# The attention of the first block spread over one stream of weight parts, a head every three slots

## What is computed

```python
proj = rms_norm(x) @ w_in                      # q (16 heads), k, v (4 heads), u, gate_a, gate_b
q, k = rms_norm(q, q_norm_g), rms_norm(k, k_norm_g)       # a head of 128 columns each
y_a  = windowed_gqa(q, k, v, attn_sink) @ w_attn_o         # per head, 256 x 256 scores, ALiBi, sink
y_b  = (y_act @ glu_w_a) * sigmoid(y_act @ glu_w_b)        # y_act: the state-space branch
merged = sigmoid(gate_a) * y_a + sigmoid(gate_b) * y_b
x = x + merged @ w_out
```

## Time and profile before

| what | value |
|---|---|
| median of 3 runs | 3993.94 us (3990.68 to 3995.81) |
| profiled execution | 3992.67 us, span 3990.9 us |
| TensorE busy (share of the span) | 2447.9 us (61%) |
| VectorE, ScalarE, GpSimd busy | 2199.8, 1252.7, 2657.1 us |
| mean granted clock of TensorE | 0.804 of full speed |

### The profile page before, as it was taken

The page is one execution under the profiler, slowest core; times in us unless marked ns, Lnnn a source line. Parts: engine busy times, 40 slices in busy tenths (PEclk is TensorE's granted clock), DMA queues, the critical chain, the costliest instruction groups (busy, mean ns, idle before and its releaser), DMA issues.

```text
span 3990.9 us, 35652 instructions
## 1 busy us (share of the span) xinstructions
PE 2447.9 (61%) x11418; PEld 2021.6 (51%) x11418; DVE 2199.8 (55%) x2700; ACT 1252.7 (31%) x1773; POOL 2657.1 (67%) x1192
## 2 busy tenths in 40 slices
PE   6899977998410110100000008999999999889997
PEld 5788755777300100100000006888888888768775
DVE  7788222131799999999999984222232222221322
ACT  4666544444200000000000003444434444333553
POOL 5200333876587877878788886777787777666555
PEclk9999987998755555555555558999999999988998
DMA  5444422664699999999999995555555555444444
GB/s 162 131 125 131 134 84 70 183 190 150 251 420 381 418 405 383 417 407 422 378 422 422 405 399 162 164 171 162 164 173 165 170 163 167 134 159 137 132 127 142
DMA packets 238655, 935.94 MB, mean 235 GB/s; under 512 B 37664, under 2 KB 39840, under 8 KB 171680
## 3 DMA queue, kind: packets, MB, share of 16 engines
q0 software_dynamic: 73728, 536.90, 32.7%
q1 hardware_dynamic: 156576, 390.13, 32.2%
q10 hardware_dynamic: 8192, 6.90, 0.6%
HBM read 927.02 MB, written 2.10 MB: 233 GB/s over the span
## 4 chain that ended last, share of the span: by engine, by line
PE 55%; DVE 21%; issue 8%; POOL 7%; ACT 3%; DMA 3%; DVEq 2%; ACTq 1%; POOLq 0%
PE products L599 39%; PE products L1131 8%; DVE arena L2416 8%; DVE arena L2404 7%; POOL arena L2136 7%; DMA arena<-peer_up_in,arena 2%; DVE arena L946 1%; PE products L620 1%; PE products L888 1%; PE products L1905 1%; PE products L1880 1%; DMA arena<-peer_down_in,arena 1%; ACT weights_high L531 1%; PE products L911 1%; ACTq L1820 1%
## 5 line engine op out<-in xcount | busy, mean ns | idle before, releaser
L543 POOL TENSOR_TENSOR weights_low<-arena,weights_high 128x1024 fp32r<-128x1024 f32 x528 | 1287.1, 2445 | 625.3 <-ACT weights_high L531 624.2
L599 PE MATMUL products<-weights_high,input_high 128*128 128x512 f32 x2432 | 991.7, 408 | 555.4 <-DVE weights_low L543 533.1
L531 ACT ACTIVATE weights_high<-arena 128x1024 fp32r<-128x1024 f32 x612 | 645.7, 1059 | 1126.2 <-PE products L599 963.8
L599 PE MATMUL products<-weights_high,input_low 128*128 128x512 f32 x2432 | 963.3, 396 | 0.0
L599 PE MATMUL products<-weights_low,input_high 128*128 128x512 f32 x2432 | 963.0, 396 | 0.0
L599 PEld LDWEIGHTS products<-weights_high,input_high 128*128 128x128 f32 x2432 | 468.3, 193 | 654.8 <-DVE weights_low L543 326.3
L2416 DVE SCALAR_TENSOR_TENSOR arena<-arena 128x2048 f32<-128x2048 f32 x256 | 611.6, 2389 | 29.4 <-DMA arena<-peer_up_in,arena 4.4
L2136 POOL DMA_INDIRECT arena<-peer_down_in,arena x256 | 507.6, 1983 | 174.3 <-DVE arena L2404 88.1
L2136 POOL DMA_INDIRECT arena<-peer_up_in,arena x256 | 552.1, 2157 | 82.6 <-issue 80.0
L2404 DVE SCALAR_TENSOR_TENSOR arena<-arena 128x2048 f32<-128x2048 f32 x256 | 573.7, 2290 | 22.5 <-DMA arena<-peer_down_in,arena 20.1
L620 PE MATMUL products<-arena 128*128 128x128 f32 x248 | 58.0, 409 | 852.8 <-DVE arena L2436 720.2
(11 more groups left out here) (311 smaller groups left out, 2913.4 us busy)
## 6 DMA issues: line engine op xcount, KB each, us to landing
arena<-dsa_in SPq DMA_DIRECT2D x320, 512.0 KB, 3.5
arena<-w_in_in SPq DMA_DIRECT2D x128, 512.0 KB, 3.8
arena<-mla_wide_in SPq DMA_DIRECT2D x97, 512.0 KB, 3.5
arena<-w_attn_o_in SPq DMA_DIRECT2D x32, 512.0 KB, 3.6
arena<-w_out_in SPq DMA_DIRECT2D x32, 512.0 KB, 4.1
arena<-peer_w_query_in SPq DMA_DIRECT2D x32, 512.0 KB, 4.4
arena<-dsa_w_out_in SPq DMA_DIRECT2D x32, 512.0 KB, 3.6
arena<-glu_w_b_in SPq DMA_DIRECT2D x16, 512.0 KB, 3.7
```

The source lines that it names most:

```text
L531: nc.scalar.activation(w_hi[:, u % RING, :, at], ring[:, u % RING, :, at], ACT.Copy).then_inc(hi_made, 1)
L543: ops.tensor_tensor(w_lo[:, u % RING, :, at], ring[:, u % RING, :, at], w_hi[:, u % RING, :, at].bitcast(F32), op=ALU.subtract).then_inc(l ...
L599: mm = nc.tensor.matmul(PS[:, bank(b) + t, 0:width], x[:, x0 + n, at], y, start=n == 0 and m == 0, stop=n == len(parts) * PK - 1 and m == 2)
```

## The change

From the value slab to the output slabs there is now one list of slots on all engines, numbered a = 0 to 135: value (0 to 7), query (8 to 39), gated (40 to 71), attention output (72 to 103), output (104 to 135). In slot a every engine does what is due: TensorE one part (`a_part`) and then steps (`a_pe`), ScalarE the weight copy four parts ahead (`hi_part`) and then `a_act`, VectorE `a_dve`.

- Head h takes its scores in slot 20 + 3h (k = 0), exponentials and normalising in the next (k = 1), transposes at k = 3, values at k = 4. The last head's values are in slot 69.
- Key turns are in slots 2 and 3. Query slab i is rooted and scaled in slot 16 + 8i and turned in the second and third slot behind; QT, like the scaled rows, is kept twice.
- The gated slabs come before the attention-output slabs. The state-space output is split in slots 33 to 36. Four pairs of attention output are split to the upper half of XH and XL (slots 37, 38, 40 and 46), four to the lower half (69 to 72).
- After a gated slab VectorE makes GB = sigmoid(gate_b) y_b; after an attention-output slab it makes GB = GB + GA y_a, with a second pair of row buffers `gate_rows`.
- The merge is turned by quarters: turns 0 to 5 in slots 97 to 102, turns 6 and 7 in slots 105 and 106.
- v_quad, sinks_quad and the wait on v_staged go. SyncE waits before it loads x until all attention output is split. Loops on the engines become straight code.

```diff
-W_U, W_G, W_K, W_V, W_Q, W_O, W_GLU, W_OUT, W_PQ = 0, 2, 10, 11, 12, 16, 20, 24, 28
+W_U, W_G, W_K, W_V, W_Q, W_GLU, W_O, W_OUT, W_PQ = 0, 2, 10, 11, 12, 16, 20, 24, 28
+A_GLU, A_O, A_OUT = PARTS * (W_GLU - W_V), PARTS * (W_O - W_V), PARTS * (W_OUT - W_V)
+A_END = A_OUT + PARTS * 4
+A_FIRST, A_SPACE = 20, 3
+def a_heads(a):
+    for h in range(HEADS):
+        k = a - A_FIRST - A_SPACE * h
+        if 0 <= k <= 4:
+            yield h, k
+def a_turn(a):
+    i, m = divmod(a - 2 * PARTS, PARTS)
+    if a in (2, 3):
+        return a - 2
+    return 2 + 2 * i + m - 2 if 0 <= i < QUADS and m in (2, 3) else None
+def a_pair(a):
+    for u in range(HEADS // 2):
+        free = A_GLU - PARTS // 2 + u if u < PARTS // 2 else A_O - PARTS + u
+        if a == max(free + 1, A_FIRST + A_SPACE * (2 * u + 1) + 5):
+            return u
+def a_merged_turn(a):
+    u = a - (A_OUT - PARTS + 1)
+    if u in range(6):
+        return u
+    return u - 2 if u in (8, 9) else None
+def a_place(u):
+    return (u + PARTS // 2) % PARTS
...
+        def a_pe(pe, a):
+            for h, k in a_heads(a):
+                if k == 3:
+                    pe.wait_ge(p_ready, after(H_A + h))
+                    pe.wait_ge(pt_ready, 1 + h)
...
+                    tr.then_inc(p_turned, 1)
+                if k == 4:
...
+                    mm.then_inc(pv_made, 1)
+            for h, k in a_heads(a):
+                if k == 0:
...
+                    pe.wait_ge(turned, after(X_Q + 2 * i + c // 2))
+                    pe.wait_ge(score_read, 1 + h)
...
+                    mm.then_inc(score_made, 1)
+            j = a_turn(a)
+            if j is not None:
+                i, u = divmod(j - 2, 2)
+                moved(pe, B_K if j < 2 else B_Q + i)
...
+        def a_act(act, a):
+            for h, k in a_heads(a):
...
+            for h, k in a_heads(a):
+                if k == 1:
+                    act.wait_ge(bias_ready, after(H_A + h))
...
+            if a == 0:
+                head_roots_of(act, B_K, W_K, 0, v_rows)
...
+            i, m = divmod(a - 2 * PARTS, PARTS)
+            if 0 <= i < QUADS and m == 0:
+                head_roots_of(act, B_Q + i, W_Q + i, 0, ks_rows)
...
+        def a_dve(dve, a):
+            if a == 0:
+                scale_heads(dve, B_K, 0, 0, ks_rows)
+            i, m = divmod(a - 2 * PARTS, PARTS)
+            if 0 <= i < QUADS and m == 0:
...
+                scale_heads(dve, B_Q + i, 1, i, rows[:, i % 2])
+            for h, k in a_heads(a):
+                if k == 1:
+                    dve.wait_ge(exp_done, after(H_A + h))
...
+                    n.then_inc(p_ready, 1)
+            for h, k in a_heads(a):
+                if k == 0:
+                    dve.wait_ge(score_made, after(S_A + h))
...
+            sp.wait_ge(lhs_lo, L_AO + HEADS // 2)
             sp.dma_start(X, I["x"][0].rearrange("(t p) d -> p t d", p=P)).then_inc(x_in, 16)
...
+            for a in range(A_OUT + PARTS // 2):
+                hi_part(act, PARTS * W_V + a + RING)
+                a_act(act, a)
...
+            for a in range(A_END):
+                a_part(pe, a)
+                a_pe(pe, a)
```

More of the change, by code:

```diff
@@ L345, in program @@
         v_rows = cols.take(NT, NC)
-        v_quad = cols.take(NT, HD)
-        QT = cols.take(QUAD, SEQ)
+        QT = cols.take(2, QUAD, SEQ)
         PA = cols.take(2, NT, SEQ)
         PTA = cols.take(2, NC)
+        gate_rows = cols.take(2, NT, NC)
         H = G.rearrange("p t d -> p (t d)")[:, 0:NT * D].rearrange("p (t d) -> p t d", t=NT)
@@ L482, in program @@
         skip_ready, y_made, y_read, y_act = sem("skip_ready"), sem("y_made"), sem("y_read"), sem("y_act")
-        merged = sem("merged")
+        gated, merged = sem("gated"), sem("merged")
         out_done = sem("out_done")
@@ L685, in scale_heads @@
                 op=ALU.mult).then_inc(evac[b % 2], 2)
[L688 to L707, removed]
-                        mm = nc.tensor.matmul(PS[:, SCORE_BANK + s % 2, at:at + seen(t)], qq[:, t * P:(t + 1) * P],
-                                              kk[:, 0:seen(t)], start=n == 0, stop=n == len(pairs) - 1)
-                    at += seen(t)
-                mm.then_inc(score_made, 1)
@@ L2203, in _ @@
-            act.drain()
-            split_hi(act, W_O, 0, range(3, RING))
-            lhs_split_hi(act, YT, range(KT // 2))
-            with act.Fori(0, 4) as i:
-                feed(act, W_O, i)
-            made(act, W_O + 3)
-            act.wait_ge(ys_in, 16 * 8 * SSM_KT)
-            for u in range(SSM_KT // 2):
-                nc.scalar.activation(XH[:, 2 * u:2 * u + 2].rearrange("p k (j i) -> p k j i", i=CHUNK),
-                                     YS[:, 2 * u:2 * u + 2].rearrange("p k (i j) -> p k j i", i=CHUNK), ACT.Copy)\
-                    .then_inc(lhs_hi, 1)
@@ L2214, in _ @@
-            with act.Fori(0, 4) as i:
-                split_hi(act, W_GLU, i, range(RING, PARTS))
-                made(act, W_GLU, i, PARTS // 2 - 1)
-                act.wait_ge(merged, 1 + i)
-                nc.scalar.activation(rows[:, 0], PS[:, bank(0):bank(0) + 2], ACT.Sigmoid).then_inc(evac[0], 2)
-                split_hi(act, W_GLU + 1, i, range(RING))
-            turn_hi(act, X_MER)
+            for a in range(A_OUT + PARTS // 2):
+                hi_part(act, PARTS * W_V + a + RING)
+                a_act(act, a)
@@ L2232, in _ @@
                           allow_slow_non_contiguous=True).then_inc(pos_in, 16)
-            with act.Fori(0, 4) as i:
-                feed(act, W_OUT, i)
+            for a in range(A_OUT + PARTS // 2, A_END):
+                hi_part(act, PARTS * W_V + a + RING)
             act.wait_ge(evac[0], B_PQ)
```

401 lines of the change are left out of this document (173 added, 228 removed).

## The result

The kernel after takes 3890.26 us (median of four runs, 3884.87 to 3893.88) where the kernel before takes 3992.31 in the same comparison: a ratio of 0.9745, with a 95% interval of 0.9727 to 0.9763. The profiled execution took 3888.33 us. The prediction was 3889, with a range of 3872 to 3914.

What follows compares the result with a forecast made beforehand. TensorE was taken to wait on VectorE and ScalarE chains and run at slow clock; 411.9 us of work plus 16.5 of waits make 428.4 in place of 532.3, 103.9 less, giving 3889 us, range 3872 to 3914.

Steps and rivals of the forecast that it cites:

- (a): Key heads: ScalarE's roots and scaling take 6.4 us with the copy, against two slots (5.44); 1.2 us lost.
- (b): Slot 24: scaling before normalising makes head 1's transposes wait 5.5 us (3.1 least, 7.1 dear end), plus 1.7 clock: 7.2.
- (c): Slots 32 to 35: third query slab's scaling ahead of head 4's scores; 1.3 us wait plus 1.7 clock, 3.0.
- (d): Slots 33 to 40: split subtractions ahead of heads 5 and 6; one head late by 2, clock 1.6: 3.6 us.
- (e): Gated stage: slot 56 carries a gated evacuation and new scores; head 12 late by 0 to 3, taken as 1.5 us.
- clock term: Half-speed products after a TensorE stop, priced from one 2.24 us stop: 1.7 us, or 1.6, per restart.
- three stage ends: Starts of gated, attention-output and output slabs: they cost nothing any more, with no wait over 1 us.
- 16 heads: Attention heads: costed at nothing, as three slots hide each chain, with weights ready some 1.5 us before TensorE asks.
- Everything hidden: Rival: chains of later terms read too slow, TensorE stands only 0 to 8 us; 3872 to 3880, chance 0.22.
- Contention at every head: Rival, third listed case: VectorE meets GpSimd throughout, twelve more heads cost 1.6 us each; 3899 to 3918, chance 0.20.
- Only the stage ends gain: Rival: the attention stretch stays as long as today, only stage ends gain 31 us; 3961, chance 0.04.
- slower case: In-order wait at every head's transposes: slower if each is late by 5.8 us or more; 7 late gives 4012; chance 0.03.

Runs made afterwards that it cites:

- best2: Kernel after with scaling behind head steps, four further moves (key roots, state-space splits, gated step, fused normalising) and a head every two slots: 3875.42 us, 0.9723 of before.
- order: Kernel after with the scaling of a query slab put behind the heads' steps in VectorE's slot: 3883.41 us, 0.9738 of the kernel before.
- space2: Kernel after with a head every two slots in place of three, still three slots from scores to transposes: 3879.97 us, 0.9721 of the kernel before.
- nosink: Kernel after with the sink left out of the softmax denominators, dropping VectorE's small add: 3876.18 us, one run, no ratio.
- twoslots: Kernel after with a head's transposes two slots behind its scores, not three: 3957.07 us, 0.9922 of the kernel before.
- second repeat: Kernel after, unchanged, measured again with the last group of experiments: 3891.98 us, 0.9763 of the kernel before.
- ends: Kernel after with all splits of the left operands back at the stage ends (slots 39 and 71): 3906.18 us, 0.9783 of the kernel before.
- mergewhole: Kernel after with all eight merge turns at once in slot 103, ahead of the output slabs: 3900.36 us, 0.9765 of the kernel before.

## Why the prediction was right

**The whole.** The sum was 411.9 of work and 16.5 of waits; the stream took 430.2, 1.8 more than the 428.4. That it is so near is partly luck: the work was priced 4.4 us too low and the waits with their restarts 2.5 us too high (14.0 found), and the two errors partly cancel. The range was meant to reach to the upper edge of the third rival, but that edge is 3918, and 3914 was written; the measured time is far from either.

**The work** was too cheap by 4.4 us. Slots without steps keep the 2.72. A slot with one head's scores and another's transposes takes 4.05, one with values 3.63, so a head costs 1.33 + 0.91 = 2.24, not 2.14 (16 x 0.10 = 1.6). A slot with a merge turn takes 3.20, so a turn costs 0.48, not 0.42 (18 x 0.06 = 1.1). Both prices came from rows in which such steps stood side by side; between slab products each handover costs a little more. The other 1.7 was not found in one place. best2's 416.1, with 0.8 of waits, says the same: 3.4 over 411.9.

**(a) The key turn**: 1.2 forecast, 1.28 found, with no slow restart behind it.

**(b) Slot 26**: 7.2 forecast, 6.26 + 2.2 = 8.5 found. Between the ends I had taken 5.5 for the wait; it is 6.26, nearer to the dear end of 7.1, and the reason is the one given for that end: two of VectorE's steps each meet a subtraction. order and space2 show that scaling ahead of normalising makes the wait. The restart: transposes, scores, a turn and the first products from 518.76 to 523.51 at half pace, 2.2 above the full-clock distances of the other heads, where 1.7 was put.

The trace shows the small add, both inputs in SBUF, at 1.93 us beside GpSimd and at 0.16 alone. That agrees with the exclusive lock in SBUF — State Buffer, "SBUF: Two separate sides", of the Trainium skill, which the prediction left as the dearer case. nosink adds what that sentence alone doesn't give: taking one operation out of the row moves the meeting to the next.

ScalarE's switch of tables between the roots and the factors, in the same slot:

```profile
511.03 1.28 ACT L717 ACT_TABLE_LOAD   x1
512.32 0.30 ACT L717 ACTIVATE arena<-arena 128x8 f32<-128x8 f32 x1
```

It takes 1.29 to the next activation. The 2.66 of the Trainium skill (ScalarE: Activation LUTs, "What ACT_TABLE_LOAD costs") would have made (b) and (c) 1.4 later; the trace goes with the shorter price.

**(c) Slot 35**: 3.0 forecast, 0.98 found; **(d) slots 33 to 40**: 3.6 forecast, 1.58 + 0.27 found; **(e) slot 59**: 1.5 forecast, 1.36 found. The waits themselves were near (1.3 and 2 in the sum for (c) and (d)). The step that failed is the clock term that I added to each, 1.7 and 1.6: the rows behind these stops show transposes of 0.66 us at a distance of 0.49 to the scores, which is full pace (granted clock 1.00). What the rows of the changed streams show is this: behind stops of 0.98 to 2.09 us TensorE went on at the full clock; behind those of 3.08 and more it ran at half pace for a while, at a cost of 1.5 to 2.5 us where it was worked out here. Between them a stop's length doesn't tell: 2.39 and 2.40 lost the clock in twoslots, 2.49 and 2.51 kept it, and in the kernel before stops of 2.24 did both. Nor does the loss begin with the stop's end: behind the 3.77 of the second repeat the transposes and scores ran at full pace, and the granted clock was 0.50 only from 577.0 to 579.0. What decides was not found. I had one row, the 2.24 of the earlier trace rows, and applied it to every stop.

**What I costed at nothing.** The supply of parts: TensorE waits for no weight part in the stream, so it is right. The three stage ends: 86.70 busy of 86.70, and no wait at the output slabs; ends and mergewhole put 14.4 and 16.0 back, of which 13 and 11.1 are the stage ends themselves. The 16 heads: right in the result, since only the four late ones of (b) to (e) wait, but the spare 1.5 us per head was counted too high. twoslots takes 2.72 away and each head is 3.5 late on the mean, where 1.5 of spare would leave 1.2. The head shown above meets GpSimd twice and is 3 us longer for it; with a third slot such meetings stay hidden, and I had counted the chain from steps at their undisturbed lengths.

**The rivals.** Everything hidden falls with the 6.26 of slot 26; but best2 shows that it was to be had, at 416.1. Contention at every head falls with four late heads in place of 16. VectorE does meet GpSimd often (in nine of the 16 heads the add takes 0.84 us or more in place of 0.16), but the third slot hides it. With two slots of distance the rival becomes true. Only the stage ends gain falls with the attention's 0.99 in the window; twoslots, in which 36 of the 102 us remain, shows what it would have looked like: 3957.07, near the 3961 given for it. The slower case needed 5.8 us of lateness at each head; the mean with two slots is 3.5, so even one slot less still leaves a kernel 0.9922 of the one before.

**A miss of the experiments' own.** For space2 I expected a loss, because I looked at how dense the heads were and not at which slots they share with other steps. The cause of (b), known by then, would have given the sign: 21 + 2h and 24 don't meet.

**Left open**: why the stream starts at 432 to 434 us in some executions and at 438 to 439 in others, which moves a whole time by as much as some of these edits; why what follows the stream, which no experiment touches, takes anything from 3013.9 us (nosink) to 3028.3 (space2); and what decides whether TensorE loses its clock behind a stop of 2.2 to 2.5 us.

## What to carry to other kernels

Before a chain of small steps is put beside a stream of large products, write down for each slot and engine which steps meet there: one pair in the wrong order cost 9 us here, and either their order in the slot or the distance of the heads removed it. A distance between producer and consumer is cheap as long as the stream has work to fill it; count the chain with one operation of the other engine per step that can meet one, not with the steps' lengths alone, since one slot too few cost 66 us. Price a stop by what rows show behind stops of its own length, and look at more than one such row: here no stop of up to 2.09 us in the changed streams brought a half-speed restart, every one of 3.08 and more did, and of those between some did and some didn't. And repeat the trace of the unchanged kernel: one head there was 2.2 us later the second time.

## What the hardware did that I had not expected

VectorE and GpSimd take turns operation by operation, so the loss depends on how many of VectorE's operations of certain kinds fall into a row of subtractions, and not on their lengths. The kinds that paid here are the adds and subtractions of two SBUF inputs, the normalising and the small bias step. The reciprocals did not (0.15 and 0.17 within a subtraction), nor did the maxima (L904): all 32 of them took 0.41 to 0.42, though 26 began within a subtraction; nor did the operations that read the scores from PSUM (L898), at 0.47 to 0.48. In slot 24 two of three met one (1.93 and 2.38, together 3.5 us over their lengths alone); with the add removed, both of two did (4.18, again 3.6 over). mergewhole's slot 38 shows the same pair of operations at 4.99. Who goes first can hang on 0.04 us, so the same kernel showed a wait of 1.58 in one trace and of 3.77 in another. And the clock is no function of the stop's length alone: stops of 2.24 us in one and the same kernel lost it once and kept it once.
